# Expert weights of an encoder block in 2 MB pieces through a ring of eleven buffers

## The reference, cut to what matters

```python
for l in range(DEPTH):                                   # 2
    m = mixing_sublayer(x, pos, ...)
    x = layer_norm(DN_ALPHA * x + m, ln_mix_g[l], ln_mix_b[l])
    f = moe_ffn(x, w_router, router_bias, exp_w_gate[l], exp_w_up[l], exp_w_down[l])
    x = layer_norm(DN_ALPHA * x + f, ln_ffn_g[l], ln_ffn_b[l])

# moe_ffn: gates = group_limited_router(x2d, ...)        # 2 of 16 experts per token
for e in range(N_EXPERTS):                               # 16
    he = jax.nn.silu(x2d @ w_gate[e]) * (x2d @ w_up[e])  # [1024, 512] each
    y = y + gates[:, e:e + 1] * (he @ w_down[e])         # [512, 1024]
```

## Time and profile before

| | |
|---|---|
| median of 3 runs | 1028.85 us (1025.39 to 1029.4) |
| the profiled execution, own time | 1029.46 us |
| its span, first to last instruction | 1027.6 us |
| mean granted TensorE clock | 0.945 of full speed |
| TensorE busy | 920.7 us (90% of the span) |
| VectorE, ScalarE, GpSimd busy | 383.9, 253.8, 296.3 us |
| moved by DMA | 268.6 MB, 261 GB/s over the span |

### The profile page before, as it was taken

The page is one execution under the profiler, slowest core; times in us unless marked ns, Lnnn a source line. Parts: engine busy times, 40 slices in busy tenths (PEclk is TensorE's granted clock), DMA queues, the critical chain, the costliest instruction groups (busy, mean ns, idle before and its releaser), DMA issues.

```text
span 1027.6 us, 15688 instructions
## 1 busy us (share of the span) xinstructions
PE 920.7 (90%) x5976; PEld 594.1 (58%) x5976; DVE 383.9 (37%) x799; ACT 253.8 (25%) x473; POOL 296.3 (29%) x253
## 2 busy tenths in 40 slices
PE   6999899599999778999999998994999978779995
PEld 5777777455555334555497777774555534345551
DVE  5996646411111101111569957464111111001115
ACT  5326623111111111111332266130111111101111
POOL 0731374022222121222335322741222221212213
PEclk9999899689999889999999989996999989889998
DMA  9621194789999999995223112846998999999932
GB/s 301 208 82 51 49 343 149 304 311 379 384 386 382 371 393 376 383 358 173 82 65 123 54 38 98 332 168 252 366 347 295 379 383 390 389 382 381 362 101 82
DMA packets 122037, 268.60 MB, mean 261 GB/s; under 512 B 8418, under 2 KB 23938, under 8 KB 121472
## 3 DMA queue, kind: packets, MB, share of 16 engines
q1 hardware_dynamic: 111136, 247.14, 65.0%
q0 software_dynamic: 10848, 20.69, 7.8%
HBM read 252.64 MB, written 21.23 MB: 267 GB/s over the span
## 4 chain that ended last, share of the span: by engine, by line
PE 60%; DVE 17%; DMA 15%; issue 3%; SPq 3%; ACT 1%; DVEq 0%
PE bank L769 17%; DMA w_up<-in_exp_w_up 14%; PE bank L424 14%; PE bank L775 11%; DVE bank L1145 7%; PE bank L768 7%; SPq L322 3%; PE bank L750 2%; PE bank L758 2%; PE bank L813 1%; PE bank L809 1%; DVE xTl L1114 1%; PE bank L570 1%; DVE w_gate L1121 1%; DVE w_gate L1122 1%
## 5 line engine op out<-in xcount | busy, mean ns | idle before, releaser
L768 PE MATMUL bank<-w_gate,moex 128*64 128x256 f32 x1376 | 322.6, 395 | 42.5 <-DMA w_up<-in_exp_w_up 42.5
L769 PE MATMUL bank<-w_up,moex 128*64 128x256 f32 x1376 | 322.6, 395 | 0.0
L768 PEld LDWEIGHTS bank<-w_gate,moex 128*64 128x64 f32 x1376 | 195.4, 143 | 92.2 <-issue 67.8
L769 PEld LDWEIGHTS bank<-w_up,moex 128*64 128x64 f32 x1376 | 195.4, 143 | 79.3 <-issue 16.6
L775 PE MATMUL bank<-w_down,moex 128*64 128x512 f32 x688 | 166.6, 605 | 0.0
L1396 DVE TENSOR_TENSOR moemem<-bank,moemem 64x256 f32<-64x256 f32 x86 | 35.4, 411 | 311.8 <-ACT moemem L1023 311.8
L1561 POOL TENSOR_TENSOR wl<-w_gate,wh 128x2048 fp32r<-128x2048 f32 x17 | 77.9, 4587 | 145.2 <-ACT wh L886 98.2
L424 PE MATMUL bank<-xTh,wh 128*128 128x512 f32 (+1 forms) x256 | 101.6, 397 | 11.4 <-DVE xTl L1114 10.1
L1023 ACT ACTIVATE moemem<-bank 64x256 f32<-64x256 f32 x86 | 32.8, 381 | 314.1 <-PE bank L768 163.1
L424 PE MATMUL bank<-xTl,wh 128*128 128x512 f32 (+1 forms) x256 | 95.6, 374 | 0.0
L424 PE MATMUL bank<-xTh,wl 128*128 128x512 f32 (+1 forms) x256 | 95.6, 373 | 0.0
(11 more groups left out here) (213 smaller groups left out, 1094.9 us busy)
## 6 DMA issues: line engine op xcount, KB each, us to landing
w_up<-in_exp_w_up SPq DMA_DIRECT2D x32, 2048.0 KB, 23.7
w_down<-in_exp_w_down SPq DMA_DIRECT2D x32, 2048.0 KB, 21.2
w_gate<-in_exp_w_gate SPq DMA_DIRECT2D x32, 2048.0 KB, 20.8
w_gate<-in_w_in SPq DMA_DIRECT2D x13, 1024.0 KB, 5.9
w_gate<-in_w_out SPq DMA_DIRECT2D x8, 1024.0 KB, 5.0
x_rows<-xtok POOLq DMA_DIRECT2D x8, 512.0 KB, 5.3
y_rows<-xtok SPq DMA_DIRECT2D x8, 512.0 KB
w_up<-y_rows SPq DMA_DIRECT2D x8, 512.0 KB, 6.0
```

The source lines that it names most:

```text
L768: m1 = pe.matmul(bank[i][CH:P, 0:256], x, wg[:, k, cols], start=(k == 0), stop=(k == KD - 1))
L769: m2 = pe.matmul(bank[i][0:CH, 0:256], x, wu[:, k, cols], start=(k == 0), stop=(k == KD - 1))
```

## The change: what it does

**Pieces.** Gate and up of an expert are joined on the host into rows of 1024 floats (up, then gate), and loaded in two halves by input row: `HIGH_K` has the blocks k = 0 to 3 of both, `LOW_K` the blocks 4 to 7. Down stays as it is. All three pieces are 2 MB in rows of 4 KB.

**Ring.** Piece number 3e + part goes into buffer (3e + part) % 11. Nine of these buffers are the slots of before, one is `xtok`, one is the new name `moew` for the memory of `xTl`. Piece i is loaded when piece i - 11 is given back: a `HIGH_K` piece after the first half of the wide products (`wide_half`), a `LOW_K` piece after the second, a down piece after `narrow`.

**Order of products.** A chunk forms the products of k = 0 to 3 for both column halves, then waits for `LOW_K`, then k = 4 to 7 for i = 0 and for i = 1.

**Chunk numbers.** TensorE reads six before the tables, six behind the table products, and the others one by one ahead of experts 0 to 4.

**Scores.** The loop over heads m is now the outer one.

```diff
+        low_at = nc.sbuf_base
+        moew = sb("moew", [P, KD * T])
+        xTl = shared("xTl", low_at, KD * T, F32R)
...
+        ring = [slot[2][0][:, :], slot[0][1][:, :], slot[0][2][:, :], slot[0][0][:, :],
+                xtok[:, :, :].rearrange("p j n -> p (j n)"), moew[:, :],
+                slot[1][0][:, :], slot[1][1][:, :], slot[1][2][:, :], slot[2][1][:, :], slot[2][2][:, :]]
+        R = len(ring)
+        HIGH_K, LOW_K, DOWN = range(3)
+        def weights(e, part):
+            return ring[(3 * e + part) % R].rearrange("p (k n) -> p k n", k=KF)
...
+        def weights_in(eng, l, e, part):
+            i = 3 * e + part
+            eng.wait_ge(wexp_in[i % R], 16 * (l * len(range(i % R, 3 * E, R)) + i // R + 1))
...
+                src = a["exp_w_down"][l * E + e] if part == DOWN else a["exp_w_wide"][l * E + e, 512 * part:512 * part + 512, :]
...
                 sp.wait_ge(ln_out, TT * (l + 1))
-                load_expert(l, 0, 0)
+                load_expert(l, 1, HIGH_K)
                 fill_choices(l)
-                load_expert(l, 2, 1)
+                load_expert(l, 3, HIGH_K)
+
+                sp.wait_ge(x1_stored, 16 * TT * (l + 1))
+                sp.wait_ge(y_filled, 16 * TT * (l + 1))
+                sp.wait_ge(tr_done, TT * (2 * l + 1))
+                load_expert(l, 1, LOW_K)
+                load_expert(l, 3, LOW_K)
 
                 sp.wait_ge(late_done, l + 1)
-                load_expert(l, 1, 2)
-                load_expert(l, 2, 2)
+                load_expert(l, 1, DOWN)
+                load_expert(l, 2, DOWN)
 
                 starts = [first_chunk(sp, l, e) for e in range(1, E - 1)]
-                for e in range(SLOTS, E):
-                    done = starts[e - SLOTS] * 2
-                    sp.wait_ge(wide_done, done)
-                    load_expert(l, e, 0)
-                    load_expert(l, e, 1)
-                    sp.wait_ge(narrow_done, done)
-                    load_expert(l, e, 2)
+                for i in range(R, 3 * E):
+                    e, part = (i - R) // 3, (i - R) % 3
+                    sp.wait_ge((wide_half, wide_done, narrow_done)[part], starts[e] * 2)
+                    load_expert(l, i // 3, i % 3)
...
-                for c in (2 * b, 2 * b + 1):
-                    for g in range(2):
-                        for m in range(4):
+                for m in range(4):
+                    for c in (2 * b, 2 * b + 1):
+                        for g in range(2):
...
-                starts = [first_chunk(pe, l, e) for e in range(E + 1)]
+                starts = [first_chunk(pe, l, e) for e in range(6)]
...
                 mm.then_inc(tab_done, 1)
+                starts += [first_chunk(pe, l, e) for e in range(6, 12)]
...
+            def widen(e, k, i):
+                w = weights(e, k // 4)[:, k % 4, :]
+                x = xgT[:, k % 4, k // 4, :]
+                return [pe.matmul(bank[i][CH * n:CH * n + CH, 0:256], x, w[:, 512 * n + 256 * i:512 * n + 256 * i + 256],
+                                  start=(k == 0), stop=(k == KD - 1)) for n in range(2)]
...
-                pe.wait_ge(wexp_in[e % SLOTS][0], loads(l, e))
-                pe.wait_ge(wexp_in[e % SLOTS][1], loads(l, e))
+                weights_in(pe, l, e, HIGH_K)
                 pe.wait_ge(xgT_set, c + (l + 1))
+                for k in range(4):
+                    for i in range(2):
+                        mms = widen(e, k, i)
+                for mm in mms:
+                    mm.then_inc(wide_half, 1)
+                weights_in(pe, l, e, LOW_K)
                 for i, done in ((0, wide_first), (1, wide_done)):
-                    for mm in widen(e, i):
+                    for k in range(4, KD):
+                        mms = widen(e, k, i)
+                    for mm in mms:
                         mm.then_inc(done, 1)
...
+                    if len(starts) <= E:
+                        starts.append(first_chunk(pe, l, len(starts)))
```

More of the change, by code:

```diff
@@ L216, in build @@
         rows_in = sem("rows_in")
-        wexp_in = [[sem(f"{n}_in{r}") for n in ("gate", "up", "down")] for r in range(SLOTS)]
+        wexp_in = [sem(f"weights_in{r}") for r in range(11)]
         dve_chain, pool_chain = sem("dve_chain"), sem("pool_chain")
@@ L252, in build @@
         xg_moved, xg_turned, xgT_set = sem("xg_moved"), sem("xg_turned"), sem("xgT_set")
-        wide_first, wide_done, narrow_done = sem("wide_first"), sem("wide_done"), sem("narrow_done")
+        wide_half, wide_first, wide_done, narrow_done = sem("wide_half"), sem("wide_first"), sem("wide_done"), sem("narrow_done")
         silu_set, he_set, he_turned, heT_set, y_set = (
@@ L281, in head @@
             return x[:, 512 * i:512 * i + 512].rearrange("p (k n) -> p k n", k=2)
-        def loads(l, e):
-            return 16 * (l * len(range(e % SLOTS, E, SLOTS)) + e // SLOTS + 1)
+        def weights_in(eng, l, e, part):
+            i = 3 * e + part
+            eng.wait_ge(wexp_in[i % R], 16 * (l * len(range(i % R, 3 * E, R)) + i // R + 1))
         @block.sync
@@ L317, in load_piece, with load_expert @@
                 sp.dma_start(dst, src).then_inc(wraw_in[n % 2], 16)
[L319 to L323, removed]
+            def load_expert(l, e, part):
+                src = a["exp_w_down"][l * E + e] if part == DOWN else a["exp_w_wide"][l * E + e, 512 * part:512 * part + 512, :]
+                sp.dma_start(weights(e, part), src.rearrange("(k p) n -> p k n", p=P)).then_inc(wexp_in[(3 * e + part) % R], 16)
             def load_choices(l):
@@ L368, in _ @@
                         sp.dma_start(xtok[:, :, :], a["x"].rearrange("(j p) n -> p j n", p=P)).then_inc(xtok_in, 16)
-                sp.wait_ge(s_done, TT * (l + 1))
+                sp.wait_ge(s_done, 4 * TT * (l + 1))
                 sp.wait_ge(gm_done, 2 * (l + 1))
@@ L373, in _ @@
                 sp.wait_ge(pt_done, TT * (l + 1))
[L374 removed]
+                load_expert(l, 2, LOW_K)
                 sp.wait_ge(gm_raw, 2 * (l + 1))
                 sp.wait_ge(conv_norm, 2 * (l + 1))
[L377 removed]
+                load_expert(l, 0, DOWN)
                 sp.wait_ge(conv_low, 2 * (l + 1))
                 sp.wait_ge(gm_low, 2 * (l + 1))
[L381 removed]
+                load_expert(l, 0, LOW_K)
                 sp.wait_ge(last_low, l + 1)
                 sp.wait_ge(piece_low, (PIECES - 1) * (l + 1))
[L385 removed]
+                load_expert(l, 2, HIGH_K)
                 sp.wait_ge(op_done, TT * (l + 1))
[L388 removed]
+                load_expert(l, 0, HIGH_K)
                 sp.wait_ge(ln_out, TT * (l + 1))
[L391 removed]
+                load_expert(l, 1, HIGH_K)
                 fill_choices(l)
[L393 removed]
+                load_expert(l, 3, HIGH_K)
[4 more added lines that the diff above has]
+                load_expert(l, 3, LOW_K)
                 sp.wait_ge(late_done, l + 1)
[L396 to L397 removed]
+                load_expert(l, 1, DOWN)
+                load_expert(l, 2, DOWN)
                 starts = [first_chunk(sp, l, e) for e in range(1, E - 1)]
[L400 to L406 removed]
+                for i in range(R, 3 * E):
+                    e, part = (i - R) // 3, (i - R) % 3
+                    sp.wait_ge((wide_half, wide_done, narrow_done)[part], starts[e] * 2)
+                    load_expert(l, i // 3, i % 3)
                 sp.wait_ge(narrow_done, starts[E - 3] * 2)
@@ L572, in scores @@
                                            kr[64 * g:64 * g + 64, 64 * c + 64 - h:64 * c + 64], start=True, stop=True)
-                mm.then_inc(s_done, 1)
+                            if m == 3:
+                                mm.then_inc(s_done, 1)
             def turn_probs(l, b):
@@ L760, in turn_hidden @@
                 mm.then_inc(he_turned, 1)
[L762 to L770, removed]
+            def widen(e, k, i):
[3 more added lines that the diff above has]
+                                  start=(k == 0), stop=(k == KD - 1)) for n in range(2)]
             def narrow(e, k):
-                wd = slot[e % SLOTS][2][:, :].rearrange("p (k n) -> p k n", k=KF)
+                wd = weights(e, DOWN)
                 return [pe.matmul(bank[5][CH * n:CH * n + CH, :], heT[:, k, :], wd[:, k, 512 * n:512 * n + 512],
@@ L789, in chunk @@
                 turn_gathered(l)
-                pe.wait_ge(wexp_in[e % SLOTS][2], loads(l, e))
+                weights_in(pe, l, e, DOWN)
                 pe.wait_ge(y_set, c + 1)
@@ L1160, in softmax_max @@
                 i = b % 2
-                dve.wait_ge(s_done, n + 1)
+                dve.wait_ge(s_done, 4 * (n + 1))
                 for g in range(2):
@@ L1745 @@
         "w_router": x["w_router"], "const": const, "mixc": mixc,
-        "exp_w_gate": x["exp_w_gate"].reshape(DEPTH * E, D, FE), "exp_w_up": x["exp_w_up"].reshape(DEPTH * E, D, FE),
+        "exp_w_wide": np.concatenate([x["exp_w_up"], x["exp_w_gate"]], axis=3).reshape(DEPTH * E, D, 2 * FE),
         "exp_w_down": x["exp_w_down"].reshape(DEPTH * E, FE, D),
```

1 line of the change is left out of this document (removed).

## The result

The changed kernel takes 975.11 us (median of 4 runs, 974.52 to 975.77) against 1028.51 us for the kernel before on the same chip (4 runs): a ratio of 0.9486, 95% interval 0.9465 to 0.9507. The forecast was 981, from 968 to 998.

A forecast was written before the change was run, and what follows sets the result against it. Weight loads up to experts 12 to 14, with DMA standstills before, were taken to set the expert stages' ends. 20.5 + 30.3 + 2.7 - 3.0 - 2.0 = 48.5 us off 1029.46 gave 981 us, range 968 to 998.

The forecast's parts named there:

- Fill of the standstill: Expert stages' weight loads: two more buffers, given back by halves, keep DMA engines running; stream gains 10.1 and 18.4 us.
- Rows of 4 KB: Gate and up loads: a 2 MB piece takes 0.32 us less, some 22 pieces, 7.0 us in each layer.
- rival (1): Gate and up loads: longer rows bring nothing, pieces stay at 5.50 us, 14 us drop out, 995 us; chance 0.12.
- Halves: Expert 12: TensorE begins at the first half, so it waits for down rather than up; inside 20.5 and 30.3 us.
- Chunk numbers: TensorE before the tables: eleven fewer reads start the first chunk 5 to 7 us sooner, counted as nothing.
- Stage ends: Ends of the two expert stages, set by expert 12's down landing plus remaining chunks: 20.5 and 30.3 us sooner.
- GpSimd's loop: Gather and scatter beside weight loads after expert 12: scatter rows wait on longer weight rows, costing 1 us a layer.
- rival (3): Scatter landing in the expert stages: GpSimd bounds every chunk, kernel slower than before, 1062 us at 2.5 us more; chance 0.05.
- The clock's 1.5 a layer: TensorE at expert 12: several shorter waits may each halve the granted clock, costing 1.5 us a layer.
- Score order: Score products in the mixing parts: neighbours in other quadrants take 65 ns a record against 78, 2.7 us in all.
- rival (2): Score products: quadrants truly run four at a time, 2.51 us becomes 0.63, 14.5 us gained, 969 us; chance 0.07.
- Rival (4): Weight stream not kept running (wait for y_filled, or SyncE late): fill of 200 to 211 half lost, 991 us; chance 0.08.

The follow-up runs named there:

- an early piece: Changed kernel with expert 3's first half loaded at half of the output projection instead of after the residual rows, in both layers: 970.34 us, ratio 0.9463.

## Why the prediction was right, and where not

**Fill of the standstill (10.1 and 18.4): right as seen, but not the ring's alone.** No dip is left. Nine buffers cost 14 us, not 28.5. In their trace the first gap is 6 us and not 11, beside late tables that end some 10 us earlier, and 740 to 797 reads 361 GB/s where before read 327. I put the whole of both down to the ring and nothing to reads and halves; what each closes by itself, in a ring of nine, no run takes apart.

**Rows of 4 KB (7.0 a layer): right.** 15 us for both. By the Trainium skill, "DMA: Bandwidth & Descriptors", Specifications, 512 bytes suffice for the line rate; here 2 KB rows move 382 and 4 KB rows 395 GB/s at about the same busy share (1.05 and 1.03), so this kernel doesn't bear it out, and rival (1) is out. The 400 GB/s that I had named as a sign is not reached by the long windows (395 and 396).

**Halves (inside the 20.5 and 30.3): right in kind.** 7.2 us. The load behind expert 2's first half was issued at +52.1 us from the first chunk (forecast +51.6) and 11.0 us ahead of its own landing (forecast 9.7). What decides whether the stream stops is another distance, that to the landing of the piece ahead: 5.8 us. My sum didn't look at it; by its own pitch it would have been 9.7 less 5.85, some 4 us.

**Chunk numbers: the step that failed.** "I count this at nothing: what hides it is the wait for weights" was true of TensorE's own time. It left out that TensorE's time gives buffers back: all reads in front cost 7.3 us with this ring, most of it in the second layer, by a queue gone dry. The remark that SyncE must issue behind late_done "by 210" was the right place with too late a time: with the issue at 205.02, 1.4 us ahead of the last landing, the next piece landed 8.5 us behind it, while 5.8 us ahead was enough in the second layer of after. The sum took no harm from this nothing, because the ring's term had already set the first chunk "some 6 us sooner" and the fill of the gap as whole; the value of the reads stood inside it, unnamed. The last six reads cost nothing.

**Stage ends: 20.5 and 30.3 less 2.5 each, measured 19.9 and 28.7.** GpSimd's loop (1 a layer) never bound: unhindered chunks follow each other in 11.76 us in every kernel above, so rival (3) is out with its 72.6 us of room. The clock's 1.5 a layer came in the first layer alone: there the narrow part behind the landing of expert 12's down piece takes 5.63 us (1.98, 0.40 and 3.25 in the chain above) where I had 4.01, in the second 4.08. The landing itself came 0.9 us earlier than forecast in the first layer and 1.5 later in the second. Windows of after, behind the wait of 1.97 us for expert 11's second half and behind that of 1.7 us for expert 12's down piece:

```profile
361.40:363.40 2.00, 2.00 (x20) 1.35 (x22) 0.00 (x0) 0.06 (x1) 0.00 (x0) 1.00 1.08 336
384.20:386.20 2.00, 2.00 (x5) 0.39 (x6) 0.00 (x0) 0.00 (x0) 0.00 (x0) 0.50 1.03 422
```

Behind the first it stays at its upper level of 2.4 GHz, behind the second, the third within expert 12's chunk, it is at 1.2 as in the earlier trace rows. So in the first layer the fall comes once at expert 12, and not with each of the short waits.

**Score order (2.7): mechanism right, size off.** 36 ns a record where I chose 65. The row I took, 16 records alternating in columns, has products over all 128 rows of the array, at the same upper clock; with 64 rows the alternation in columns alone gives 49. That is also below the 53 that I set against rival (2) as what two at a time would give, so 53 was no floor. The time is 5.8 us for both layers. Rival (2) named 14.5 us: the Trainium skill, "TensorEngine Tiling (Array Packing)", Key Properties, says that tiles work independently of each other; the trace agrees only in part, since four quadrants in turn give 2.2 times the speed of one (78 to 36 ns a record), not four.

**Rival (4), the stream not kept running, is out:** SyncE's wait for y_filled is in the trace, but pieces were still in the queue. A stream that stops is what the versions with a late first chunk and those with an early piece showed.

The sum missed by 6 us, all of it towards too slow: 3.1 from the scores; 2.0 from GpSimd's deduction and 1.4 from the clock's in the second layer, less 0.6 by which the landings were late in sum. Each term but the scores came within 2 us, so the hit in the range is not one of errors that cancel.

## What to carry to other kernels

Price an instruction on an engine that has slack also by what it gives back: with a ring, a consumer that is 6.5 us later gives its buffers back later, and a transfer queue that runs dry costs some 4 to 5 us beyond the wait itself (an estimate: 9.0 to 10.4 us from issue to landing, less the 5.2 of a piece behind others). Look for the tightest give-back by its distance to the landing of the piece ahead (here an expert with two chunks, 5.8 us) before an improvement ahead of it is counted; of two that fill the same gap only their joint effect can be forecast. Products that use a quadrant of the array are to be ordered so that neighbours lie in other rows and other columns.

## What the runs showed of the hardware

At the upper clock, the records of 64 x 64 products (two to a product, mostly 128 columns) follow each other in 36 ns when they take turns over the four quadrants, in 49 when in rows or columns alone, in 78 when four in a row use one quadrant. At equal busy share the DMA engines moved 3 to 4% more with rows of 4 KB than with 2 KB. A lone 2 MB piece issued on a dry queue landed after 9.0 to 10.4 us (732.34 to 741.36, 746.42 to 756.84); behind others, the same piece landed 5.2 us after its forerunner, and the six that landed from 355.7 to 384.1 us came 5.7 apart on average. A read of a chunk number costs TensorE 0.61 us of its idle time ahead of the tables, and nothing visible between chunks, which stay 11.76 us apart.
